# Mamba-style scan steps of a hybrid transformer kernel: the eight decay differences of each step go from VectorE to ScalarE

## The reference, cut to what matters

```python
a_cs = jnp.cumsum(a, axis=-1)                      # running sum inside chunks of 128 tokens
decay_in = segsum_exp(a_cs)                        # exp(a_cs[l] - a_cs[s]) for s <= l, else 0
cb = jnp.einsum("bclgn,bcsgn->bcgls", Cc, Bc)
y_diag = jnp.einsum("bcgls,bcgjls,bcsgjp->bclgjp", cb, decay_in, xdt)
states = jnp.einsum("bclgn,bcgjl,bclgjp->bcgjpn", Bc, exp(a_cs[..., -1:] - a_cs), xdt)
...                                                # carry the states over the four chunks -> prev
y_off = jnp.einsum("bclgn,bcgjpn,bcgjl->bclgjp", Cc, prev, exp(a_cs))
y = (y_diag + y_off) + d_skip * xs
return rmsnorm(y * silu(z), norm_w)
```

## Time and profile before

| | us |
|---|---|
| median of 3 runs (3382.36 to 3388.52) | 3386.4 |
| the profiled execution's own time | 3385.07 |
| its span, first to last instruction | 3383.6 |
| TensorE busy | 3097.3 |
| VectorE busy | 1908.9 |
| ScalarE busy | 909.4 |
| GpSimd busy | 1904.5 |
| mean granted TensorE clock, share of full | 0.959 |

### The profile page before, as it was taken

How to read it: one execution, slowest core, us unless ns; L and a number is a source line. 1 busy time by engine, 2 the same in 40 slices (tenths; PEclk the granted TensorE clock), 3 DMA queues, 4 the chain that set the end, 5 groups by cost and what they waited for, 6 DMA issues and landing times.

```text
span 3383.6 us, 39580 instructions
## 1 busy us (share of the span) xinstructions
PE 3097.3 (92%) x15146; PEld 2404.3 (71%) x15146; DVE 1908.9 (56%) x2809; ACT 909.4 (27%) x1435; POOL 1904.5 (56%) x1860
## 2 busy tenths in 40 slices
PE   8889989989999889899999999998889898798897
PEld 5677767768777778677787677776677776586675
DVE  6755786751385569676217533335788888512313
ACT  5222213430232220243203232323343333301102
POOL 5555556547675546555567655554455555276461
PEclk9999999999999999899999999999999999999997
DMA  5222222133222222211432222221112122232221
GB/s 192 88 94 94 75 75 75 63 117 125 100 100 89 98 75 89 73 63 66 154 112 89 85 72 78 76 77 66 63 63 75 63 75 75 85 112 87 71 92 59
DMA packets 61069, 294.55 MB, mean 87 GB/s; under 512 B 5680, under 2 KB 10672, under 8 KB 31440
## 3 DMA queue, kind: packets, MB, share of 16 engines
q1 hardware_dynamic: 36384, 247.48, 20.8%
q10 hardware_dynamic: 24496, 44.54, 3.8%
HBM read 274.10 MB, written 16.84 MB: 86 GB/s over the span
## 4 chain that ended last, share of the span: by engine, by line
PE 61%; DVE 28%; ACT 5%; issue 2%; POOL 2%; DMA 1%; DVEq 0%; ACTq 0%; POOLq 0%
PE bank L396 52%; DVE bank L1908 5%; DVE h_lo L1664 2%; DVE rec_ex L2249 1%; DVE rec_cum L2206 1%; POOL w_lo L2430 1%; DVE bank L1735 1%; PE bank L735 1%; DVE rec_small L2235 1%; PE bank L752 1%; PE bank L744 1%; PE bank L924 1%; DVE last_z L2378 1%; POOL w_hi L2428 1%; DVE newton L1643 1%
## 5 line engine op out<-in xcount | busy, mean ns | idle before, releaser
L396 PE MATMUL bank<-h_hi,w_lo 128*128 128x512 f32 x3712 | 1529.0, 412 | 85.7 <-DVE h_lo L1664 34.9
L396 PE MATMUL bank<-h_lo,w_hi 128*128 128x512 f32 x3712 | 1472.6, 397 | 0.0
L396 PE MATMUL bank<-h_hi,w_hi 128*128 128x512 f32 x3712 | 1472.3, 397 | 0.0
L2428 POOL TENSOR_SCALAR w_hi<-w_raw 128x512 fp32r<-128x512 f32 x928 | 675.2, 728 | 1339.3 <-PE bank L396 1279.8
L2430 POOL TENSOR_TENSOR w_lo<-w_raw,w_hi 128x512 fp32r<-128x512 f32 x928 | 1252.2, 1349 | 77.4
L396 PEld LDWEIGHTS bank<-h_hi,w_lo 128*128 128x128 f32 x3712 | 714.9, 193 | 315.0 <-issue 51.7
L396 PEld LDWEIGHTS bank<-h_hi,w_hi 128*128 128x128 f32 x3712 | 712.5, 192 | 156.7
L396 PEld LDWEIGHTS bank<-h_lo,w_hi 128*128 128x128 f32 x3712 | 714.2, 192 | 152.3 <-issue 12.8
L965 ACT ACTIVATE raw<-bank 128x512 f32<-128x512 f32 x148 | 88.5, 598 | 383.5 <-PE bank L396 353.6
L1908 DVE SCALAR_TENSOR_TENSOR bank<-cfm_up,par,bank 128x512 f32<-128x512 f32 x232 | 175.4, 756 | 8.3
L2066 DVE TENSOR_TENSOR xT<-bank,xT 128x512 f32<-128x512 f32 x32 | 22.1, 691 | 221.7 <-PE bank L396 221.0
(11 more groups left out here) (335 smaller groups left out, 2875.3 us busy)
## 6 DMA issues: line engine op xcount, KB each, us to landing
w_raw<-in_wall SPq DMA_DIRECT2D x230, 1024.0 KB, 4.9
x_scratch<-xT ACTq DMA_DIRECT2D x12, 1024.0 KB, 4.9
xT<-x_scratch ACTq DMA_DIRECT2D x12, 1024.0 KB, 7.4
ssd_abc<-acs_scratch ACTq DMA_DIRECT2D x16, 512.0 KB, 3.5
first_xin<-in_x SPq DMA_DIRECT2D x4, 1024.0 KB, 10.7
out<-last_rows ACTq DMA_DIRECT2D x4, 1024.0 KB, 4.2
w_raw<-in_wall SPq DMA_DIRECT2D x8, 256.0 KB, 10.2
raw<-in_wpp ACTq DMA_DIRECT2D x16, 128.0 KB, 2.6
```

What stands on the lines that cost most here:

```text
L396: mm = t.matmul(bank[BANK[u]][:, :], w[:, CS16[k]], h[:, k, :], start=(k == 0 and w is m.w_lo[b]), stop=(k == KT - 1 and w is m.w_hi[b] an ...
L2428: g.tensor_scalar(m.w_hi[b][:, part], m.w_raw[b][:, part], 1.0, 1.0, ALU.mult, ALU.mult).then_inc(*s.hi.inc(u, n))
```

## The change

The eight differences of each step are no longer made by VectorE as min(abc - cur, 0), but by ScalarE as Relu(bias - abc), with the negated input (`scale=-1.0`) and the head's running sum as the per-partition bias; the Exp that follows takes `scale=-1.0`, so the value is the same. ScalarE's eight instructions stand between `tot` and the Exp, and wait in addition for the near product of the step before, since they overwrite `dec`.

In the same edit ScalarE's order is cut anew. The opening of the next step's x (`open_x`: the half and the tanh of `acc`) is now called from `next_x`, directly behind the square of the step's output, so it stands ahead of the copies out of PSUM that used to come first: `evac(x1)` and `evac(z1)` at the end of a pair, and `evac(a0)` in i = 3. The square goes into a new SBUF tile `ysq` and no longer into the PSUM tile `half`. On VectorE the copy `cur` moves from ahead of the convolution to behind `xsT`, and `gz` from behind the mask to ahead of it. The rest of VectorE's order, and TensorE's, stays.

```diff
--- before.py
+++ after.py
@@ -279,7 +279,7 @@
         self.cur, self.tot = t("cur", [P, 3, NC, 2]), t("tot", [P, 2, NC])
         self.xsT, self.xdt, self.xdd = t("xsT"), t("xdt", [P, NC, P]), t("xdd", [P, NC, P])
         self.st = t("st", [P, NC - 1, P])
-        self.gz, self.eo = t("gz"), t("eo")
+        self.gz, self.eo, self.ysq = t("gz"), t("eo"), t("ysq")
         inner = m.at
         m.at = m.norm.end
         self.s = [t(f"s{q}", [SSD_H, T]) for q in range(8)]
@@ -1083,22 +1083,29 @@
         a.wait_ge(*s.acs.at(l))
         load_decays(0)
 
-        def convolve(i, g):
-            j, z = i + 4 * g, 2 * g + 1
+        def open_x(i, g):
             a.wait_ge(*dve.at("acc", l, i, g))
             silu_parts(q.acc[:, :], q.half[:, :], q.th[:, :], "xs", l, i, g)
+
+        def open_z(i, g):
             a.wait_ge(*dve.at("xs", l, i, g))
-            a.wait_ge(*act.at("evac", UNIT["z", l, j]))
-            silu_parts(m.raw[z], q.half[:, :], q.th[:, :], "z", l, i, g)
+            a.wait_ge(*act.at("evac", UNIT["z", l, i + 4 * g]))
+            silu_parts(m.raw[2 * g + 1], q.half[:, :], q.th[:, :], "z", l, i, g)
 
         def decay(i, g):
-            n = 2 * i + g
+            n, j = 2 * i + g, i + 4 * g
             a.wait_ge(*s.abc.at(l, n))
-            a.wait_ge(*dve.at("dec", l, i, g))
             a.wait_ge(*act.now())
             a.activation(q.tot[:, :, :], q.abc[:, :, P - 1:T:P], ACT.Exp).then_inc(*act.inc("tot", l, i, g))
-            a.wait_ge(*act.now())
-            a.activation(q.dec[:, :, :], q.dec[:, :, :], ACT.Exp).then_inc(*act.inc("dec", l, i, g))
+            if n:
+                a.wait_ge(*pe.at("diag", l, (n - 1) // 2, (n - 1) % 2))
+            for hh in range(2):
+                for c in range(NC):
+                    a.wait_ge(*act.now())
+                    a.activation(q.dec[:, hh, CS[c]], q.abc[:, hh, CS[c]], ACT.Relu, scale=-1.0,
+                                 bias=q.tok[:, 1, c, 2 * j + hh:2 * j + hh + 1]).then_inc(*act.inc())
+            a.wait_ge(*act.now())
+            a.activation(q.dec[:, :, :], q.dec[:, :, :], ACT.Exp, scale=-1.0).then_inc(*act.inc("dec", l, i, g))
             for hh in range(2):
                 a.wait_ge(*act.now())
                 a.activation(q.eo[64 * hh:64 * hh + 64, :], q.abc[64 * hh:64 * hh + 64, hh, :],
@@ -1107,31 +1114,41 @@
                 a.wait_ge(*act.now())
                 load_decays(n + 1)
 
-        def output(i, g):
+        def square_y(i, g):
             a.wait_ge(*dve.at("yv", l, i, g))
-            a.wait_ge(*act.now())
-            a.activation(q.half[:, :], m.y[:, i + 4 * g, :], ACT.Square).then_inc(*act.inc("ysq", l, i, g))
-
+            if 2 * i + g:
+                a.wait_ge(*dve.at("ysum", l, (2 * i + g - 1) // 2, (g + 1) % 2))
+            a.wait_ge(*act.now())
+            a.activation(q.ysq[:, :], m.y[:, i + 4 * g, :], ACT.Square).then_inc(*act.inc("ysq", l, i, g))
+
+        def next_x(i, g):
+            a.wait_ge(*dve.at("silu", "z", l, i, g))
+            open_x(*((i, 1) if g == 0 else (i + 1, 0)))
+
+        open_x(0, 0)
         for i in range(3):
             x0, z0, x1, z1 = ssd_after(l, i)
-            convolve(i, 0)
+            open_z(i, 0)
             decay(i, 0)
             evac(x0, m.raw[0])
-            output(i, 0)
-            convolve(i, 1)
+            square_y(i, 0)
+            next_x(i, 0)
+            open_z(i, 1)
             evac(z0, m.raw[1])
             decay(i, 1)
-            output(i, 1)
+            square_y(i, 1)
+            next_x(i, 1)
             evac(x1, m.raw[2])
             evac(z1, m.raw[3])
         a0, g0 = ssd_after(l, 3)
-        convolve(3, 0)
+        open_z(3, 0)
         decay(3, 0)
-        output(3, 0)
+        square_y(3, 0)
+        next_x(3, 0)
         evac(a0, m.raw[0])
-        convolve(3, 1)
+        open_z(3, 1)
         decay(3, 1)
-        output(3, 1)
+        square_y(3, 1)
         evac(g0, m.raw[1])
         rstd(m.rs_ssd[:, :], q.th[:, :], "ssd", l)
 
@@ -1821,20 +1838,17 @@
 
         def convolve(i, g):
             j, x = i + 4 * g, 2 * g
-            v.wait_ge(*dve.now())
-            v.tensor_copy(q.cur[:, :, :, :], q.tok[:, :, :, 2 * j:2 * j + 2]).then_inc(*dve.inc())
             v.wait_ge(*act.at("evac", UNIT["x", l, j]))
             conv(m.raw_m[x], lambda k: par1(m, "conv_w", j * SSD_K + k), par1(m, "conv_b", j), i, g)
+
+        def open_x(i, g):
             silu(q.xsT[:, :], q.half[:, :], q.th[:, :], "xs", l, i, g)
             dve.mark("xs", l, i, g)
 
-        def decay(i, g):
-            v.wait_ge(*s.abc.at(l, 2 * i + g))
-            for hh in range(2):
-                for c in range(NC):
-                    v.wait_ge(*dve.now())
-                    v.tensor_scalar(q.dec[:, hh, CS[c]], q.abc[:, hh, CS[c]], q.cur[:, 1, c, hh:hh + 1], 0.0, ALU.subtract,
-                                    ALU.min).then_inc(*dve.inc("dec", l, i, g))
+        def tokens(i, g):
+            j = i + 4 * g
+            v.wait_ge(*dve.now())
+            v.tensor_copy(q.cur[:, :, :, :], q.tok[:, :, :, 2 * j:2 * j + 2]).then_inc(*dve.inc())
             xps = bank[2][:, :].rearrange("p (c h d) -> p (c h) d", h=2, d=SSD_HD)
             v.wait_ge(*pe.at("xt", l, i, g))
             for dst, n, name in ((q.xdd, 2, "xdd"), (q.xdt, 0, "xdt")):
@@ -1842,14 +1856,15 @@
                 v.tensor_tensor(dst[:, :, :].rearrange("p c (h d) -> p (c h) d", h=2), xps,
                                 q.cur[:, n, :, :].rearrange("p c h -> p (c h)").unsqueeze(2).to_broadcast(
                                     [P, NC * 2, SSD_HD]), ALU.mult).then_inc(*dve.inc(name, l, i, g))
+
+        def decay(i, g):
+            silu(q.gz[:, :], q.half[:, :], q.th[:, :], "z", l, i, g)
             v.wait_ge(*act.at("dec", l, i, g))
             v.wait_ge(*dve.now())
             v.tensor_tensor(q.dec[:, :, :], q.dec[:, :, :], q.cbm[:, g, :, :].rearrange("p c n -> p (c n)").unsqueeze(
                 1).to_broadcast([P, 2, T]), ALU.mult).then_inc(*dve.inc("decm", l, i, g))
-            silu(q.gz[:, :], q.half[:, :], q.th[:, :], "z", l, i, g)
-
-        def output(i, g):
-            j = i + 4 * g
+
+        def states(i, g):
             v.wait_ge(*pe.at("states", l, i, g))
             v.wait_ge(*dve.now())
             v.tensor_copy(q.st[:, 0, :], bank[3][:, 0:P]).then_inc(*dve.inc())
@@ -1862,12 +1877,18 @@
                     v.scalar_tensor_tensor(q.st[:, c, hs], q.st[:, c - 1, hs], q.tot[:, hh, c:c + 1],
                                            bank[3][:, c * P + 64 * hh:c * P + 64 * hh + 64], ALU.mult,
                                            ALU.add).then_inc(*dve.inc("st", l, i, g))
+
+        def near(i, g):
+            j = i + 4 * g
             v.wait_ge(*pe.at("diag", l, i, g))
             if 2 * i + g == 0:
                 v.wait_ge(*s.xs.at("x", l))
             v.wait_ge(*dve.now())
             v.scalar_tensor_tensor(m.y[:, j, :], q.xsT[:, :], par1(m, "d", j), bank[5][:, :], ALU.mult, ALU.add).then_inc(
                 *dve.inc())
+
+        def far(i, g):
+            j = i + 4 * g
             v.wait_ge(*pe.at("off", l, i, g))
             v.wait_ge(*act.at("eo", l, i, g))
             v.wait_ge(*dve.now())
@@ -1876,14 +1897,24 @@
             v.tensor_tensor(m.y[:, j, P:T], m.y[:, j, P:T], bank[4][:, P:T], ALU.add).then_inc(*dve.inc())
             v.wait_ge(*dve.now())
             v.tensor_tensor(m.y[:, j, :], m.y[:, j, :], q.gz[:, :], ALU.mult).then_inc(*dve.inc("yv", l, i, g))
+
+        def square_y(i, g):
             v.wait_ge(*act.at("ysq", l, i, g))
-            add_square(q.half[:, :], "ysum", l, i, g)
-
-        for i in range(4):
-            for g in range(2):
-                convolve(i, g)
-                decay(i, g)
-                output(i, g)
+            add_square(q.ysq[:, :], "ysum", l, i, g)
+
+        order = [(i, g) for i in range(4) for g in range(2)]
+        convolve(0, 0)
+        open_x(0, 0)
+        for n, at in enumerate(order):
+            tokens(*at)
+            decay(*at)
+            states(*at)
+            near(*at)
+            far(*at)
+            square_y(*at)
+            if n < 7:
+                convolve(*order[n + 1])
+                open_x(*order[n + 1])
         v.wait_ge(*pe.at("ms", "ssd", l))
         rstd_sum(q.th[:, :], bank[2][:, :], 1.0 / SSD_W, "ssd", l)
         rstd(m.rs_ssd[:, :], q.th[:, :], "ssd", l)
```

More of the change, by code:

```diff
@@ L1823, in convolve @@
             j, x = i + 4 * g, 2 * g
+            v.wait_ge(*act.at("evac", UNIT["x", l, j]))
+            conv(m.raw_m[x], lambda k: par1(m, "conv_w", j * SSD_K + k), par1(m, "conv_b", j), i, g)
+        def open_x(i, g):
+            silu(q.xsT[:, :], q.half[:, :], q.th[:, :], "xs", l, i, g)
+            dve.mark("xs", l, i, g)
+        def tokens(i, g):
+            j = i + 4 * g
             v.wait_ge(*dve.now())
             v.tensor_copy(q.cur[:, :, :, :], q.tok[:, :, :, 2 * j:2 * j + 2]).then_inc(*dve.inc())
[L1826 to L1829, removed]
```

(7 more changed lines are left out.)

## The result

The changed kernel takes 3413.4 us (median of 4, 3410.8 to 3413.8) against 3385.8 us, a ratio of 1.0079 with a 95% interval of 1.0063 to 1.0094: 0.8% slower. The forecast was 3414 us, in a range of 3402 to 3424.

The account below looks back on a forecast made before the run. TensorE, busy 92% of the span, was taken as the bound. Stalls 18.0, clock 9.0, running sum 2.7 and differences -2.2 gave +27.5 us on a profiled 3385.1 us; with the median 1.3 above, 3414 us, range 3402 to 3424.

Parts of the forecast that it names:

- The copies behind next_x: Scan steps: late copies out of PSUM stall TensorE 3.0 us before x0, x0 and a0 in each layer, +18.0 us.
- The clock: Behind each of the six new TensorE gaps, matmuls run at the low clock for a time: 1.5 us each, +9.0 us.
- their clock cost is not there: Rival: the six stalls come but the granted clock stays at its upper level behind them; 3403 us, chance 0.10.
- the clock stays low twice as long: Rival: the low clock behind each of the six stalls lasts twice as long; +40 us, 3426 us, chance 0.06.
- The running sum and `cur`: Way to turn of (i,1), i < 3: SBUF sum waits for GpSimd, outweighing the removed cur copy; six times +0.45, +2.7 us.
- The differences: Step (3,1): without VectorE's differences xdd and states start sooner; -1.1 us a layer, -2.2 in all.
- The relief decides: Rival: the late evac(x1) is no stall, leaving only the shorter way to turn; -7.5 us, 3379 us, chance 0.07.
- The Relus bound the steps: Rival: slow Relus or table reloads on ScalarE delay odd steps' near products; 3416 to 3418, or 3430 us and more, chance 0.05.

Follow-up runs that it names:

- evac_first: The changed kernel with evac(x1) and evac(z1) again ahead of next_x at the end of a pair: 3385.9 us, ratio 1.0002.
- stall_only: The kernel before with only ScalarE's order changed, the next x's half and tanh ahead of evac(x1) and evac(z1): 3419.3 us, ratio 1.0106.
- square_psum: evac_first with the square written to the PSUM tile half again, so the sum of squares has one SBUF input: 3379.1 us, ratio 0.9979.
- relu_only: The kernel before with only the differences moved to ScalarE's eight Relus, all orders and the PSUM square kept: 3384.6 us, ratio 0.9998.
- evac_near: evac_mid with evac(x1) one VectorE instruction sooner, before the next convolution's end: 3396.2 us, ratio 1.0026.
- evac_mid: The changed kernel with evac(x1) between the wait for the next convolution and the half and tanh: 3408.4 us, ratio 1.0068.
- conv_ahead: The changed kernel with the next convolution in VectorE's idle time, next_x ahead of the square, evac(x1) directly behind decay(i,1): 3335.6 us, ratio 0.9851.

## Why the prediction was right, and where it was only near

**The copies behind next_x** were the large term, 18.0 us for six stalls. They are there, six of them in the places named, at 3.17 us instead of 3.0: 19.0 us, which is the loss for the reason given. The 0.17 us are small terms not counted, among them the square, 0.63 us into SBUF where 0.60 was taken from PSUM. evac_first and stall_only show the cause from both sides.

**The clock** was put at 1.5 us a gap, 9.0 in all, and is the term that was too small. The 48 matmuls behind the six gaps took 0.3, 3.0, 1.6, 1.8, 2.9 and 1.6 us too long, 11.1 us together, 1.9 a gap. The rivals "their clock cost is not there" and "the clock stays low twice as long" both happened, at single gaps.

**The running sum and `cur`** was put at +0.45 us for six steps. L1667 took 1.71 us, and the waits at L496 of i < 3 grew from 13.5 to 15.2 us a layer, 0.57 each, 3.4 us against 2.7. square_psum takes 1.04 us off each wait and shows the cause; what is left, 4.0 us, is 0.5 below the 4.5 of before, near the 0.6 that the prediction gave for the missing `cur` copy alone. The Trainium skill says that a VectorE instruction with two SBUF inputs contends with a GpSimd instruction that reads SBUF (SBUF — State Buffer, Who interferes with whom). The trace agrees: the sum took 0.69 us with one input in PSUM, also while GpSimd was in L2461, and 1.71 us with both in SBUF where GpSimd had started 0.14 us sooner.

**The differences** were put at -1.1 us a layer. `states` of (3,1) starts sooner as said, the wait falling by 1.54 us, and the decays come "just in time", as said. The near product came 1.45 us sooner behind `turn` (7.54 us instead of 8.99), not 1.1, as less of the quarter unit ran at the low clock than was reckoned. What the step left out is `st`, which stands behind the mask in VectorE's order: the far product waits 0.73 us, so that 0.7 us a layer are left. relu_only puts the net at 0.6. A Relu took 0.40 us and 0.03 between two, eight in 3.45 us, as taken, and no table load stands between Relu and Exp in the steps. The estimate of 0.39 us from the Trainium skill's figures (ScalarE: Activation LUTs, What ACT_TABLE_LOAD costs) is as near.

**The relief decides** is refuted by the six waits at L396 themselves; relu_only shows besides that VectorE, free of the differences, leaves L496 at 19.5 us. **The Relus bound the steps** is refuted by evac_first and by the 0.40 us of a Relu.

**Two amounts that the sum did not have.** They nearly cancel, so that the total came within 1 us of the median is in part luck. In the profiled executions the scan steps cost more than the sum. The chain gives two points in each kernel: the earlier trace rows have 24 matmuls at 134.64, the changed kernel has them at 134.71, and behind the second layer's steps the piece at 1243.74 us of before stands at 1276.62. A third point is further on (before, then the changed kernel):

```profile
1243.74 5.47 PE bank L396 x24
1896.06 2.97 PE bank L396 x12
```

```profile
1276.62 5.49 PE bank L396 x24
1924.10 2.96 PE bank L396 x12
```

That is 32.8 us between the first two points, not 27.5. The idle terms are 19.0 + 3.2 - 1.6 = 20.6, so 12.2 us are clock and restart, 2.0 a stall, where the sum had 9.0. By about 1900 us, 4.8 us have come back. In stall_only it is 4.5, in evac_near 4.1, in relu_only 1.7, in evac_mid 1.1, in evac_first 0.9, and 3.8 in conv_ahead, which has none of the stalls: the amount does not go with the gaps. It arises between about 1800 and 1908 us of before, around the norm ahead of the second block. That stretch took 101.8 us instead of 106.0, with TensorE busy for 93.8 us instead of 95.7 and a mean granted clock of 0.97 instead of 0.95. The forecast had nothing there, no run was made for it, and its cause is open.

## What to carry to other kernels

An engine that is idle for 73% of the span can still be the one that holds everything up, because its queue is strict: before an instruction that waits is moved ahead in such a queue, list what is now behind it and when each of those is needed. Here two copies of 0.6 us, moved behind a wait of 4 us, cost 0.8%, while the work that the change was about was worth 0.6 us a layer, too little to tell, as nearly all of it is hidden behind matmuls on either engine. And the largest wait of the bounding engine should be read for what it consists of: the convolution in it could be done before, and with that and the copies in their place the kernel was 1.5% faster than before the change.

## What the runs showed of the hardware that was not expected

In the scan steps' traces, the granted clock stayed at its upper level behind all six gaps of 1.0 us in TensorE's work; of the gaps of 1.8 us four of six were followed by the lower level, of those of 3.2 us five of six, in the same kernel and at the same place of the loop. So from 1.8 to 1.0 us a gap, 12 us of time came back (14 by the ratios) where 5 us of idle time went. From 3.2 to 1.8 us it was 5 us (4 by the ratios) where 8 went, but there the two intervals overlap, so that this second figure is not clear of noise.
